# Gated linear attention: the widest level's decays made by ScalarE from the cumulated gates

## The reference, cut to what matters

```
b = cumsum(a)                                  # inside a chunk
scores[i, j] = sum_d q[i, d] k[j, d] exp(b[i, d] - b[j, d])      # i >= j
o = scores @ v + (q * exp(b)) @ state
state' = exp(b_last) * state + (k * exp(b_last - b))^T @ v
```

## Time and profile before

| what | value |
|---|---|
| time, median of 3 runs | 2560.06 us (2558.01 to 2564.32) |
| the profiled execution: time, span | 2562.7 us, 2560.8 us |
| mean granted clock of TensorE | 0.986 of full speed |
| busy: PE, PEld, DVE, ACT, POOL | 2479.1, 2376.7, 1063.5, 520.1, 907.3 us |
| 360 to 545 us: PE, DVE, ACT, POOL busy (sum of five windows) | 156.6, 145.2, 100.7, 77.9 us |

### The profile page before, as it was taken

One profiled execution on the slowest core, in us unless ns is written; L12 is line 12 of the kernel. 1 busy time (PEld: TensorE's weight loads), 2 busy tenths in 40 slices (PEclk: granted clock), 3 DMA queues, 4 the chain that ended last, 5 costly groups with the idle time before them and its releaser, 6 DMA issues.

```text
span 2560.8 us, 40356 instructions
## 1 busy us (share of the span) xinstructions
PE 2479.1 (97%) x16293; PEld 2376.7 (93%) x16293; DVE 1063.5 (42%) x1653; ACT 520.1 (20%) x1118; POOL 907.3 (35%) x449
## 2 busy tenths in 40 slices
PE   7999998899999999999998999999999999999998
PEld 6899987789999999999998888678999999999998
DVE  5321228855433333333336555516533333333333
ACT  5432136532100000000003442123200000000000
POOL 4322335333334443343344331201433433434332
PEclk9999998999999999999999999999999999999999
DMA  6111132131111111111111311310111111111112
GB/s 213 44 42 34 58 116 67 51 146 45 39 50 49 49 49 41 49 46 44 49 42 58 149 33 64 124 67 9 51 49 50 41 49 49 41 49 49 41 43 73
DMA packets 41138, 154.53 MB, mean 60 GB/s; under 512 B 4800, under 2 KB 11584, under 8 KB 38864
## 3 DMA queue, kind: packets, MB, share of 16 engines
q1 hardware_dynamic: 33456, 116.49, 14.0%
q10 hardware_dynamic: 7584, 36.63, 3.8%
HBM read 134.77 MB, written 18.33 MB: 60 GB/s over the span
## 4 chain that ended last, share of the span: by engine, by line
PE 89%; DVE 6%; ACT 2%; issue 2%; DMA 1%; DVEq 0%; ACTq 0%; SPq 0%
PE bank L660 26%; PE bank L662 25%; PE bank L661 25%; PE bank L858 1%; PE bank L1284 1%; PE bank L686 1%; PE bank L1257 1%; DVE x_lo L1852 1%; PE bank L1254 1%; PE bank L1145 1%; PE bank L726 1%; PE bank L746 1%; DVE xt L1842 1%; PE bank L1279 1%; PE bank L734 1%
## 5 line engine op out<-in xcount | busy, mean ns | idle before, releaser
L660 PE MATMUL bank<-x_hi,w_hi 128*128 128x344 f32 (+1 forms) x3272 | 1060.7, 324 | 12.8 <-DVE x_lo L1876 5.5
L662 PE MATMUL bank<-x_hi,w_lo 128*128 128x344 f32 (+1 forms) x3272 | 1046.3, 320 | 0.0
L661 PE MATMUL bank<-x_lo,w_hi 128*128 128x344 f32 (+1 forms) x3272 | 1046.2, 320 | 0.0
L542 POOL TENSOR_TENSOR w_hi<-w_raw,zero 128x1024 fp32r<-128x1024 f32 x176 | 339.7, 1930 | 1445.7 <-PE bank L662 1404.6
L660 PEld LDWEIGHTS bank<-x_hi,w_hi 128*128 128x128 f32 x3272 | 618.5, 189 | 26.7 <-issue 22.9
L661 PEld LDWEIGHTS bank<-x_lo,w_hi 128*128 128x128 f32 x3272 | 618.0, 189 | 2.1 <-issue 0.5
L662 PEld LDWEIGHTS bank<-x_hi,w_lo 128*128 128x128 f32 x3272 | 618.4, 189 | 0.0
L544 POOL TENSOR_TENSOR w_lo<-w_raw,w_hi 128x1024 fp32r<-128x1024 f32 x176 | 433.3, 2462 | 13.8
L2196 DVE TENSOR_TENSOR hid<-sil,bank 128x344 f32<-128x344 f32 x132 | 67.6, 513 | 775.3 <-PE bank L662 740.3
L660 PE MATMUL bank<-hid_hi,w_hi 128*128 128x344 f32 x1056 | 339.7, 322 | 1.2 <-issue 1.2
L661 PE MATMUL bank<-hid_lo,w_hi 128*128 128x344 f32 x1056 | 337.7, 320 | 0.0
(11 more groups left out here) (308 smaller groups left out, 1793.3 us busy)
## 6 DMA issues: line engine op xcount, KB each, us to landing
w_raw<-in_w SPq DMA_DIRECT2D x187, 512.0 KB, 3.5
h<-in_x SPq DMA_DIRECT2D x3, 1376.0 KB, 8.8
h_spill<-h ACTq DMA_DIRECT2D x1, 4128.0 KB, 11.4
h<-h_spill ACTq DMA_DIRECT2D x1, 4128.0 KB, 13.5
out_y<-h ACTq DMA_DIRECT2D x3, 1376.0 KB, 5.6
g_spill<-ring ACTq DMA_DIRECT2D x6, 516.0 KB, 2.6
h<-in_x ACTq DMA_DIRECT2D x1, 3096.0 KB, 9.8
st_ring<-in_state SPq DMA_DIRECT2D x4, 768.0 KB, 4.3
```

The source lines that it names most:

```text
L542: nc.gpsimd.tensor_tensor(w_hi[:, s], w_raw[:, s], zero[:].broadcast_to([P, 1024]), ALU.add).then_inc(s_whi, 1)
L660: pe.matmul(out, wh, xh, start=(i == 0), stop=False)
L661: pe.matmul(out, wh, xl, start=False, stop=False)
L662: mm = pe.matmul(out, wl, xh, start=False, stop=(i == n - 1))
```

## The change

The seventh level (l = 6) no longer passes through GpSimd. GpSimd's loop runs over six levels, so it makes 24 pairs of differences in place of 28, and `s_df` counts six per head. For l = 6 ScalarE makes two copies of the reference column of every block, scaled by +1/16 and -1/16, into a new tile `b_mid`; it signals them on `s_bs` (which now counts two per head) and waits for that signal itself; and then it runs sixteen exponentials of 64 columns, lower and upper half of each of the eight blocks, each straight from `b_cum` into `dec` with its column of `b_mid` as the bias. Two waits come with it: on the product three steps back (it stood in GpSimd's list) and, from head 1 on, on the same level's exponentials of the head before, which read `b_mid`.

```diff
+        b_mid = at("b_mid", [P, 2, NBLK], O_S + 1664)
...
-                for l in range(NLEV):
+                for l in range(NLEV - 1):
                     n = NSTEP * hh + l
...
             def decays(hh, l):
                 n = NSTEP * hh + l
-                if l < NLEV:
-                    act.wait_ge(s_df, NLEV * hh + l + 1)
+                if l < NLEV - 1:
+                    act.wait_ge(s_df, (NLEV - 1) * hh + l + 1)
                     nc.scalar.activation(dec[:, n % 3], dec[:, n % 3], ACT.Exp, scale=1.0 / TAU).then_inc(s_ex, 1)
                     return
                 if n >= 3:
                     act.wait_ge(s_mu, n - 2)
                 b_cum = b_cums[hh % 2]
+                if l == NLEV - 1:
+                    if hh >= 1:
+                        act.wait_ge(s_ex, NSTEP * (hh - 1) + NLEV)
+                    nc.scalar.activation(b_mid[:, 0], b_cum[:, HD - 1::P], ACT.Copy, scale=1.0 / TAU)
+                    nc.scalar.activation(b_mid[:, 1], b_cum[:, HD - 1::P], ACT.Copy, scale=-1.0 / TAU).then_inc(s_bs, 1)
+                    act.wait_ge(s_bs, 2 * hh + 1)
+                    for b in range(NBLK):
+                        for half in range(2):
+                            cols = slice(b * P + HD * half, b * P + HD * (half + 1))
+                            op = nc.scalar.activation(dec[:, n % 3, cols], b_cum[:, cols], ACT.Exp, scale=(-1.0, 1.0)[half] / TAU,
+                                                      bias=b_mid[:, half, b:b + 1])
+                    op.then_inc(s_ex, 1)
+                    return
...
-                act.wait_ge(s_bs, hh + 1)
+                act.wait_ge(s_bs, 2 * hh + 2)
```

## The result

The changed kernel takes 2579.11 us (median of six runs, 2573.07 to 2579.77) against 2559.68 us for the kernel before, timed beside it (2557.40 to 2564.32). The ratio is 1.0075, 95% interval 1.0065 to 1.0086: slower by 19.4 us, where +13.2 was forecast. The profiled execution took 2579.77 us (span 2577.9, mean granted clock 0.982 against 0.986).

The account below looks back on a forecast made before the run. VectorE and TensorE alternate in the attention heads; VectorE waits for ScalarE before level 6 in three of four. Block 10.7 + split 1.5 + clock 1 = +13.2 us on 2560.06 gives 2573, range 2563 to 2582.

Parts of the forecast that it names:

- start to start of 0.241: ScalarE's level 6 block: assumed spacing in us of the sixteen 64-column exponentials, making the block 4.37 us against 1.06.
- the split: Head 3: GpSimd's split of the next weight unit starts earlier, beside VectorE's level 3 products: +1.5 us.
- The block's sum: ScalarE's longer level 6 block over four heads: +1.4, +3.3, +3.3 and +2.7, together 10.7 us (5.1 to 14.0).
- head 3's 0.56 us: Head 3, before level 6's scores: slack TensorE has to give, so the block costs +2.7 there.
- upper end of 2.9: Head 3's level 3 merge: 2.9 us late if each product half is held to the end of one split.
- lower figure of 1.1: Head 3's split: lower end of its cost in us under the rule of exclusively held shared ports.
- The clock: TensorE's granted clock, falling in widened gaps (up to +5 us) against present low stretches moving or shrinking: +1 us.
- Rival 2: Clock adds its own price: every widened gap pulls it down, present low stretches stay; +17.4 us, 2577, chance 0.14.
- GpSimd's side: Four pairs of differences go from GpSimd, one a head; their going was to bring nothing by itself.
- Cheap exponentials: ScalarE's short exponentials are cheap: block costs +1.9, sum 5.1, split does not matter; 2565 us, chance 0.13.
- GpSimd as what the next head waits for: Head boundaries: without level 6 GpSimd reaches the next head sooner, ScalarE's waits shrink; 2548 us, chance 0.05.
- the rest of the span would be unchanged: Outside the four heads: a sign of being right, beside the heads' stretch growing about 13 us.

Follow-up runs that it names:

- e3: Changed kernel, level 6's block in its own buffer, in heads 1 to 3 before the outputs' normalization; GpSimd's weight split held until head 3's level-6 product: 2550.95 us, 0.9967.
- e2: Changed kernel with one 1024-column exponential in place of the two copies and sixteen short ones, GpSimd still without level 6: 2562.20 us, ratio 1.0011.
- e9: Changed kernel with one exponential in place of copies and sixteen, and GpSimd's weight split held until head 3's level-6 product: 2555.21 us, ratio 0.9989.
- e6: Kernel before, only ScalarE's order changed: in heads 1 to 3 level 6's exponential comes right after level 5's: 2551.94 us, ratio 0.9976.
- e7: Changed kernel with eight exponentials of 128 columns in place of sixteen, GpSimd's weight split held until head 3's level-6 product: 2562.13 us, ratio 1.0013.
- e8: Changed kernel with thirty-two exponentials of 32 columns in place of sixteen, GpSimd's weight split held until head 3's level-6 product: 2582.15 us, ratio 1.0095.

## Why the prediction was right, and where it was off

**Direction and mechanism: right.** The engine that VectorE waits for at level 6 was ScalarE, and its block grew from 1.07 to 4.30 us; 4.37 was worked out. The start to start of 0.241, taken from the last step's exponentials, measured 0.240. VectorE's idle time before the product is 1.19 us in head 0 and 4.46 in heads 1 and 2, where 1.4 and 4.5 were named. e3 and e2 show the mechanism: with the same block out of VectorE's way, or with one exponential in its place, the loss is gone. By heads, the shortfall lies at the end: VectorE starts head 3's level 2 product 10.7 us later than before (497.27 against 486.58), of which 0.5 was there at the first scores of head 0, so three heads cost 10.2 where 8.0 of block was counted. Head 3 with what follows in it costs 9.8, where 2.7 and the split's 1.5 were counted.

**The block's sum: 10.7 forecast, +9.0 in the chain of runs.** This is within the uncertainty. One piece of it failed: head 3's 0.56 us that TensorE was to absorb. Its level 6 scores took 3.78 us at the lower clock, and VectorE then waited 3.35 for the turned outputs, where it had waited 0.74:

```profile
529.30 0.75 DVE L2087 SCALAR_TENSOR_TENSOR o_a<-bank,gain,g_rows 128x512 f32<-128x512 f32 x1 [3.35 <-PE bank L899]
```

**The split: +1.5 taken, +7.4 measured (5.6 in the other pair).** This is the term furthest off. The number holds what the clock does behind the collision too. The step named the right place and the right collision. VectorE's two level 3 products took 1.69 and 2.84 us beside the split, and end 0.55 us after each half of it. From the first one's start at 501.42 to the merge, which the trace has at 505.79, are 4.37 us, where 0.6 for each half had been counted: 3.2 late, just above the upper end of 2.9. So that end was the one to take. (The step's 494.4 for the end of the second half is a slip: 490.0 + 2.34 + 0.08 + 2.36 is 494.8, which its 2.9 fits; for its lower figure of 1.1 it gives no working.) The Trainium skill (SBUF — State Buffer, section "SBUF: two separate sides") says that a VectorE operation with two SBUF inputs and a GpSimd operation that reads SBUF exclude each other from a shared pair of ports for a whole instruction. The ends 0.55 us behind each half agree with that. What the step left out altogether is behind it: TensorE stands 2.97 us for the late merge, its clock is down from 508.4 to 511.6, and level 3's scores take 2.72 in place of 2.04.

**The clock: +1 taken, +5.6 measured, with some 4 us of uncertainty.** The prediction saw that the widened gaps would probably pull the clock down, and that VectorE would see part of it, up to +5. It then set as much against that for the present low stretches moving away. They did not, on the whole: over the heads the mean clock is 0.87 after and 0.90 before. Rival 2, in which the clock adds its own price (2577), was thus nearer to what happened, in this term and in the total. That the forecast's total of 2573 came within 6 us of the measured 2579 is in part luck: split and clock were 10.5 us too low together, and against that the block's sum was 1.7 too high and GpSimd's side gave 2.8 back, which had been put at nothing. That gain is at the edge of what the runs can tell, and its cause stays open. It does not show up to head 3's level 6 product, which VectorE starts at 502.24 us in e9 and at 502.18 in the kernel before. In the window from 484 to 551 us e9's clock is at its upper level, as e6's is, where the kernel before has 0.92. (The "sixteen score products" of the forecast are eight products in sixteen records; the times that it took from them hold.)

**The rivals.** Cheap exponentials (2565) fall by the block's 4.30 us. GpSimd as what the next head waits for (2548) falls twice: it stood 18.69 us for the next gates, where it had stood 10.83, and e6, with GpSimd's work unchanged, gains as much as e3. The four heads were to grow by about 13 us and grew by 20.5. That the rest of the span would be unchanged is not refuted: its 3.5 us less are within what executions of one kernel differ by.

## What to carry to other kernels

Work moved to another engine is paid for by its place in that engine's order, not by the engine's busy time: the same sixteen exponentials left the kernel 0.46% slower than before where they stood behind the outputs' scaling, and 0.33% faster where they stood ahead of the outputs' normalization. Before moving work, look whether the engine's present instruction there is already waited for, and try the reordering alone: on the kernel before, it was worth 0.24% without any of the change. When a gap in front of TensorE grows, price the products behind it at the lower clock too, and when an engine is relieved, ask what its next instruction now stands beside.

## What the runs showed of the hardware

- A ScalarE exponential with a bias operand has a fixed share of about 0.19 us from start to start beside 0.83 ns a column: 0.293 us at 128 columns (e7) and 0.240 at 64 (the changed kernel), so (0.293 - 0.240)/64 and 0.240 - 64 x 0.00083. The 0.212 at 32 columns (e8) fits that line to 0.002.
- The eight score products of a level take 3.78 us at the lower clock and 2.05 at the upper one, at the same place of the same head, without and with 3.84 us of filler before them. Filler of no use made the kernel faster than the idle gap (1.0024 against 1.0046, the intervals overlapping a little).
- A float32 matmul of 128x128 is two records in the profile, 115 ns from start to start: 40 calls came out as 80 records and 9.20 us.
